# Row halves in MLA, four quarters in RWKV-7, DA's rotation by exchanged loads, moved squares and fills in a two-layer mixer kernel

## Chip, cores and metric

One core of one Trainium2 chip. The metric is the time of one execution of the whole program in device microseconds, the median of several runs. TensorE (PE) multiplies matrices, VectorE (DVE), ScalarE (ACT) and GpSimd (POOL) work element by element, and SyncE (SP) issues DMAs. Each engine works through its own instructions in order; semaphores order the engines among each other.

## What is computed

Two layers over x of 512 tokens by 2048, all in float32. Cut from the reference:

```python
for l in range(DEPTH):                      # 2
    h = rms_norm(x, norm_g[l])
    p = h @ w_in[l]                         # 2048 columns of z, and four groups of heads
    z, p_rw, p_ml, p_mla, p_da = _split(p, IN_WIDTHS)
    y = concat(beta0 * rwkv7(p_rw), beta1 * mlstm(p_ml), beta2 * mla(p_mla), beta3 * diff_attn(p_da))
    x = x + (y * silu(z)) @ w_out[l]
# mla: q, k = [128 columns, 64 rotary columns]; softmax(q k^T, causal) v
# diff_attn: q, k = 2 maps of 64 columns per head, the first 16 columns of each rotated:
def apply_rope(x, cos, sin):
    x1, x2 = x[..., :half], x[..., half:]
    return jnp.concatenate([x1 * c - x2 * s, x2 * c + x1 * s], axis=-1)
# rwkv7, per step: S = S w + (S kk)(kk a) + v k;  y = S r   (done in chunks of 64 tokens)
```

## The kernel before

**The large products.** `x @ w_in` (256 steps a layer: 16 groups of 512 columns by 16 slices of k) and `y @ w_out` (64 steps, in column blocks of 512) are three products each of a high and a low part in fp32r: high by high, low by high, high by low. SP loads a step's weights (`raw`, L711), POOL makes the high part (`w_hi`, L728; in the first groups and the last steps of a layer ACT does, L1228, `high_part`) and the low part (`w_lo`, L738). A step's four tiles (m = 0 to 3) are three matmuls of 128x512 each, into the four banks of `ps_proj` (L769 for `w_in`, L784 for `w_out`).

**The fills.** The four mixers (MLA `la`, RWKV-7 `rw`, mLSTM `ml`, differential attention `da`, in this order, in each layer) run beside the large products. Wherever PE would wait in a mixer, `fill(name, h)` puts in so many tiles of the large products; the table `FILL` gives the counts, `planned()` deals the tiles out in order, so that a tile more here is one less elsewhere. ACT and DVE run the same plan: where a tile is the last of its group, ACT copies the bank out (L1218 `evacuate`, store L1221), and where it is the last of a column block of `w_out`, DVE adds it to x (L1644 `add_tile`). The first tile of the next group or column block waits for that copy or addition. The first three quarters of k of `w_out` run inside the DA stage, in four column blocks of 12 steps.

**Places that the change touches.**
- Start of layer 0 (L835, L1276 to L1335, L1667 to L1698): x arrives in four loads (L693), ACT squares each tile of 128 tokens in two halves (L1276), DVE and ACT make the roots, PE spreads them (L839), DVE scales the turned x, ACT and DVE split it, and the first product of `w_in` (L769) can start. The first `high_part` comes after the first `h_hi`.
- MLA, per head (L904 to L925): scores are, for each of four tiles i of 128 queries, a product over 128 rows (L919), one over the 64 rotary rows (L920, rows `own` = the half of the head) and a mask product in bf16 (L921). All have 128(i+1) columns but the mask (128).
- RWKV-7, for each pair of heads (hp = 0 to 3) (L945 to L1102): the factors (DVE) are turned (L956 to L958), copied out by ACT (L1455 to L1457), v is turned (L963), gram products (L974), the first [gk v] products (L992, two quarters of the array), five levels of an inverse (L1010 to L1031), the last of which is L1038 to L1040, then [a, state term] (L1047, `ps[q, h]`, again on the two quarters q to q), copied by ACT for both heads (L1483), then 96 small matmuls of the chunks' insides (L1057 to L1074, 192 records) and the states, one chunk after another (L1084, fill `rw_state` between).
- DA, per head (L1153 to L1189): sums of squares (L1160, L1162), a product of q and of k with the rotation matrix (L1164, L1165), DVE's multiplication by sine and cosine (L1965 to L1970), scores in two halves (L1176), ACT's exponentials (L1591), DVE's sums (L1982, L1983), then turned (L880).

An f32 matmul stands in the trace as two records.

Of the kernel before, what the change touches and what calls it, by code (L numbers as in the profile page):

```python
# [86 lines left out]
def tiles_of(g):  # L87
# [9 lines left out]
    begin=4, la_first=36, la_sums=18, la_v=4, la_heads=(7, 7, 7, 7), la_qk=(15, 11, 12, 11),  # L97
    la_probs=(13, 13, 13, 13), la_turned=(3, 3, 3, 3), la_gate=(4, 4, 4, 4),
    rw_first=8, rw_lora=(10, 10, 10, 9), rw_factors=(31, 31, 31, 33), rw_turned=(4, 4, 4, 4), rw_v=(2, 2, 2, 2),
    rw_gram=(4, 4, 4, 4), rw_x=(2, 2, 2, 2), rw_level=(1, 1, 1, 1), rw_step=(1, 1, 1, 1), rw_levels=(1, 1, 1, 1),  # L100
    rw_pu=(1, 1, 1, 1), rw_local=(5, 5, 5, 5), rw_state=(1, 1, 1, 1), rw_state_last=(1, 1, 1, 1),
    rw_carried=(2, 2, 2, 2), rw_mean=(3, 3, 3, 3), rw_gate=(13, 14, 13, 12),
    ml_first=25, ml_qk=(15, 10, 10, 10), ml_s=(8, 7, 7, 6), ml_h=(14, 13, 12, 11), ml_gate=(12, 12, 12, 12),
    da_first=21, da_sums=(14, 10, 10, 10), da_scores=(6, 6, 6, 6), da_half=(12, 17, 18, 15), da_turned=(3, 3, 3, 3),
# [4 lines left out]
for _name, _n in (("rw_mu", 13), ("rw_w0", 4), ("rw_a0", 4), ("rw_v0", 4), ("rw_k_k", 4), ("rw_k_a", 4),  # L109
                  ("rw_r_k", 4), ("rw_ln_w", 4), ("rw_ln_b", 4), ("ml_conv_w", 32), ("ml_conv_b", 8),  # L110
                  ("ml_norm_g", 4), ("mla_q_norm_g", 3), ("mla_kv_norm_g", 2), ("mla_q_g", 2),
                  ("mla_k_g", 2), ("da_q_g", 1), ("da_k_g", 1), ("da_sub_g", 1), ("norm_g", 16),
# [8 lines left out]
for _name, _n in (("ident", P), ("ones", P), ("bones", P), ("eps", 2),  # L121
# [3 lines left out]
                  ("rot_da", P), ("cos_da", T), ("sin_da", T),  # L125
# [6 lines left out]
LA_CONST = (CONST["rot_mla"][0], CONST["rot_da"][0])  # L132
DA_CONST = (CONST["rot_da"][0], CONST["causal"][0])
ML_CONST = (CONST["causal"][0], N_CONST)


def constants():
# [43 lines left out]
    put("rot_da", rotation(P, 8, 64))  # L181
    cs, sn = tables(16)
    cd, sd = np.ones((P, T), np.float32), np.zeros((P, T), np.float32)
    for b in (0, 64):
        cd[b:b + 16], sd[b:b + 16] = np.concatenate([cs, cs]), np.concatenate([sn, sn])
# [15 lines left out]
def parameters(given):  # L201
# [8 lines left out]
    for layer in range(DEPTH):  # L210
# [10 lines left out]
        for name in ("da_q_g", "da_k_g"):  # L221
            for half in range(2):
                put(name, layer, given[name][layer:layer + 1], 64 * half)
        for at, name in ((0, "ml_i_b"), (32, "ml_f_b")):
            put("gate_bias", layer, given[name][layer:layer + 1], at)
# [6 lines left out]
def planned():  # L232
# [27 lines left out]
    for h in range(4):  # L260
# [8 lines left out]
        for name in ("rw_levels", "rw_pu", "rw_local"):  # L269
            place(name, h)  # L270
# [47 lines left out]
def build(nc, a, out):  # L318

    with ExitStack() as ctx:  # L320
# [141 lines left out]
        la_mx, la_sum = rg(NT), rg(NT)  # L462
        rot_mla = const("rot_mla", la_const, LA_CONST[0])
# [5 lines left out]
        rot_da = const("rot_da", da_const, DA_CONST[0])  # L469
# [9 lines left out]
        da_qk = carve(da_p_at, 2, T)  # L479
        da_a = rg(NT, T)  # L480
# [166 lines left out]
        s_da_rotated = sem("da_rotated")  # L647
# [29 lines left out]
        for layer in range(DEPTH + 1):  # L677
# [9 lines left out]
            with nc.Block() as block:  # L687
# [54 lines left out]
                def _(pe):  # L742
# [88 lines left out]
                    for k in range(4):  # L831
                        for i in range(NT):
                            if not tail and k == 0:
                                pe.wait_ge(s_x_loaded[i], 16)
# [1192 lines left out]
```

## Time and profile before

| | |
|---|---|
| median of 3 runs | 2431.85 us (2427.43 to 2432.5) |
| the profiled execution's own time | 2427.41 us |
| its span, first to last instruction | 2425.6 us |
| PE busy | 2351.5 us (97%) |
| POOL busy | 1732.2 us (71%) |
| DVE busy | 1158.1 us (48%) |
| ACT busy | 634.4 us (26%) |
| mean granted TensorE clock | 0.993 |
| DMA, mean over the span | 117 GB/s |

The page gives for each engine the time in which it had an instruction in flight. Matmuls are pipelined, so the time that one takes is read from start to start.

### The profile page before, as it was taken

The numbers are of one execution on the slowest core, as the hardware profiler recorded it, in microseconds if no ns is written. First come the engines' busy times: TensorE is split into PE (matmuls) and PEld (weight loads), VectorE is DVE, ScalarE is ACT, GpSimd is POOL, SyncE is SP. The second block draws the span as 40 slices with busy tenths as digits, with TensorE's granted clock in tenths as the row PEclk, the third lists the DMA queues.
The fourth block names the chain that finished last, engine by engine and source line by source line (L and its number), as shares of the span: only waits on it lengthen the run. The fifth ranks groups of instructions, "written<-read, shape, count | busy, mean of one in ns | idle before, by whom it ended". The sixth has DMA issues, their size and how long they took to land. (4 is left out here: it accounts for less than half of the span.)

```text
span 2425.6 us, 38853 instructions
## 1 busy us (share of the span) xinstructions
PE 2351.5 (97%) x16320; PEld 1770.0 (73%) x16320; DVE 1158.1 (48%) x1505; ACT 634.4 (26%) x1124; POOL 1732.2 (71%) x1228
## 2 busy tenths in 40 slices
PE   7999999999999999999999999999999999999999
PEld 5767677777777677777777677777777777777777
DVE  5123345557463675454250232466475547745442
ACT  4222222121221222333241223222122212324321
POOL 3676688668587778777637666877596787888774
PEclk9999999999999999999999999999999999999999
DMA  4623243233233435632445232533232243474223
GB/s 153 189 78 100 79 152 117 75 89 104 81 105 119 127 111 192 218 86 68 140 110 166 79 109 88 157 97 97 67 113 84 84 142 112 133 252 140 79 73 123
DMA packets 163568, 284.18 MB, mean 117 GB/s; under 512 B 28408, under 2 KB 35960, under 8 KB 161856
## 3 DMA queue, kind: packets, MB, share of 16 engines
q1 hardware_dynamic: 108352, 180.93, 26.6%
q10 hardware_dynamic: 55040, 100.77, 12.1%
q8 instruction: 128, 2.10, 0.4%
q14 instruction: 48, 0.39, 0.0%
HBM read 229.97 MB, written 51.64 MB: 116 GB/s over the span
## 5 line engine op out<-in xcount | busy, mean ns | idle before, releaser
L728 POOL TENSOR_SCALAR w_hi<-raw 128x512 fp32r<-128x512 f32 x552 | 903.7, 1637 | 490.8 <-PE ps_proj L769 404.7
L738 POOL TENSOR_TENSOR w_lo<-raw,w_hi 128x512 fp32r<-128x512 f32 (+1 forms) x640 | 832.8, 1302 | 155.0 <-ACT w_hi L1228 99.5
L769 PE MATMUL ps_proj<-h_hi,w_hi 128*128 128x512 f32 (+1 forms) x1760 | 734.8, 418 | 8.0 <-ACT stage L1218 5.0
L769 PE MATMUL ps_proj<-h_lo,w_hi 128*128 128x512 f32 (+1 forms) x1760 | 690.0, 392 | 0.0
L769 PE MATMUL ps_proj<-h_hi,w_lo 128*128 128x512 f32 x1728 | 676.9, 392 | 0.0
L769 PEld LDWEIGHTS ps_proj<-h_hi,w_hi 128*128 128x128 f32 (+1 forms) x1760 | 330.3, 188 | 112.4 <-issue 26.3
L769 PEld LDWEIGHTS ps_proj<-h_lo,w_hi 128*128 128x128 f32 (+1 forms) x1760 | 330.2, 188 | 74.1
L769 PEld LDWEIGHTS ps_proj<-h_hi,w_lo 128*128 128x128 f32 x1728 | 326.3, 189 | 68.7 <-issue 11.1
L784 PE MATMUL ps_proj<-w_hi,h_hi 128*128 128x512 f32 x448 | 184.6, 412 | 9.6 <-DVE arena L1644 9.2
L784 PE MATMUL ps_proj<-w_hi,h_lo 128*128 128x512 f32 x448 | 176.3, 393 | 0.0
L784 PE MATMUL ps_proj<-w_lo,h_hi 128*128 128x512 f32 x448 | 175.8, 392 | 0.0
L784 PEld LDWEIGHTS ps_proj<-w_hi,h_hi 128*128 128x128 f32 x448 | 85.0, 190 | 31.5 <-issue 14.1
L1218 ACT ACTIVATE stage<-ps_proj 128x512 f32<-128x512 f32 (+1 forms) x118 | 70.5, 597 | 136.2 <-PE ps_proj L769 113.8
L769 PE MATMUL ps_proj<-w_hi,h_hi 128*128 128x512 f32 x256 | 104.9, 410 | 0.0
L769 PE MATMUL ps_proj<-w_lo,h_hi 128*128 128x512 f32 x256 | 99.8, 390 | 0.0
L769 PE MATMUL ps_proj<-w_hi,h_lo 128*128 128x512 f32 x256 | 99.8, 390 | 0.0
L784 PEld LDWEIGHTS ps_proj<-w_lo,h_hi 128*128 128x128 f32 x448 | 85.0, 190 | 19.7 <-issue 3.4
L784 PEld LDWEIGHTS ps_proj<-w_hi,h_lo 128*128 128x128 f32 x448 | 84.8, 189 | 18.3
L1717 DVE TENSOR_REDUCE arena<-ps 128x1 f32<-128x128 f32 (+3 forms) x96 | 47.1, 490 | 85.6 <-PE ps L921 60.6
L1228 ACT ACTIVATE w_hi<-raw 128x512 fp32r<-128x512 f32 (+1 forms) x88 | 48.7, 561 | 148.1 <-PE ps_proj L769 75.5
L1263 ACT ACTIVATE arena<-ps 128x512 f32<-128x512 f32 x24 | 14.4, 598 | 242.7 <-PE ps L1102 129.0
L1591 ACT ACTIVATE arena<-ps,arena 128x128 f32<-128x128 f32 (+3 forms) x64 | 38.7, 615 | 129.5 <-DVE arena L1718 129.5
(347 smaller groups left out, 3160.0 us busy)
## 6 DMA issues: line engine op xcount, KB each, us to landing
raw<-in_w_in_dram SPq DMA_DIRECT2D x480, 256.0 KB, 2.7
raw<-in_w_out_dram SPq DMA_DIRECT2D x128, 256.0 KB, 3.0
projected<-stage ACTq DMA_DIRECT2D x116, 256.0 KB, 2.8
arena<-projected ACTq DMA_DIRECT2D x90, 256.0 KB, 3.1
out_dram<-arena ACTq DMA_DIRECT2D x7, 1024.0 KB, 4.8
gated_hi<-arena ACTq DMA_DIRECT2D x24, 256.0 KB, 2.7
gated_lo<-arena ACTq DMA_DIRECT2D x24, 256.0 KB, 3.2
h_hi<-gated_hi SPq DMA_DIRECT2D x8, 768.0 KB, 12.9
```

Of the source, the lines that this page charges most:

```text
L728: nc.gpsimd.tensor_scalar(hi, src, 1.0, None, ALU.mult).then_inc(s_hi_split, 1)
L738: nc.gpsimd.tensor_tensor(lo, src, hi.bitcast(F32), ALU.subtract).then_inc(s_raw_split, 1)
L769: last = mm(ps_proj[rows, m, :], lhsT, rhs, start=(k == 0 and j == 0), stop=(k == KT - 1 and j == len(products) - 1))
L784: last = mm(bank[:, i, :], lhsT, rhs, start=(first and j == 0), stop=(last_k and j == 2))
L1218: nc.scalar.activation(stage[0:rows, m, :], ps_proj[0:rows, m, :], ACT.Copy).then_inc(s_proj_copied, 1)
L1228: nc.scalar.activation(w_hi[:, at_all % N_SPLIT, 0:width], raw[:, at_all % N_RAW, 0:width], ACT.Copy).then_inc(s_hi_by_act, 1)
L1263: link(nc.scalar.activation(dst, src, ACT.Ln, scale=1.0 / n, bias=eps))
L1591: nc.scalar.activation(da_p[:, b, 0:(i + 1) * P], ps[:, b, 0:(i + 1) * P], ACT.Exp, scale=da_rq[:, 4 * half + b:4 * half + b + 1], bias=da ...
L1717: link(v.tensor_reduce(mx[:, b:b + 1], ps[:, b, 0:(i + 1) * P], AX, MAX))
```

## The change

1. MLA: the rotary products of a head's four query tiles come in one block behind the four main products, two of them on the head's own half of the rows and two on the other half, for which DVE copies the rotated q across (`la_qs`), and `la_kp` is made on all rows. The four mask products come last.
2. RWKV-7: [a, state term] and the first [gk v] run on all four quarters of the array, for which the second head's turned factors are copied with their halves exchanged (three ACT copies for one); the last level loses its product with the identity; [a, state term] of the two heads is copied by ACT and DVE, one each; a fill stands between the two halves of the chunks' insides (`rw_outer`).
3. DA: no product with the rotation matrix. ACT loads the exchanged rows with four small DMAs per head (`load_da_swapped`), for the next head ahead of the exponentials of the second half; DVE multiplies them by a signed sine and an exchanged gain.
4. Start of layer 0: x is turned tile by tile; the first tile's squares come before the wait for the constants, the first `high_part` before the copies of the mean.
5. ACT's tanh of the RWKV-7 lora comes ahead of the fill `to_k`; PE turns v after the first of ACT's copies; `FILL` has other counts.

```diff
-    la_qk=(15, 11, 12, 11), rw_factors=(31, 31, 31, 33), rw_turned=(4, 4, 4, 4), rw_pu=(1, 1, 1, 1), rw_local=(5, 5, 5, 5), rw_state_last=(1, 1, 1, 1)
+    la_qk=(17, 11, 13, 11), rw_factors=(31, 33, 33, 33), rw_turned=(3, 3, 3, 3), rw_pu=(2, 2, 2, 2), rw_local=(4, 4, 4, 4), rw_outer=(1, 1, 1, 1), rw_state_last=(0, 0, 0, 0)
-    ml_qk=(15, 10, 10, 10), ml_h=(14, 13, 12, 11), ml_gate=(12, 12, 12, 12), da_half=(12, 17, 18, 15)
+    ml_qk=(19, 10, 10, 10), ml_h=(14, 14, 13, 11), ml_gate=(7, 12, 12, 12), da_half=(12, 17, 15, 16)
...
                             mm(ps[:, i, ks], la_q[:, qs], la_k[:, ks], start=True, stop=False)
-                            mm(ps[:, i, ks], la_qp[own, qs], la_kp[own, ks], start=False, stop=False)
+                        for i, rows, q_pe in ((0, own, la_qp), (1, other, la_qs), (3, own, la_qp), (2, other, la_qs)):
+                            qs, ks = slice(i * P, (i + 1) * P), slice(0, (i + 1) * P)
+                            mm(ps[:, i, ks], q_pe[rows, qs], la_kp[rows, ks], start=False, stop=False)
+                        for i in range(NT):
+                            qs = slice(i * P, (i + 1) * P)
                             mm(ps[:, i, qs], mask_ident, neg, start=False, stop=True).then_inc(s_scores_mm, 1)
...
+                            for lower, upper in ((slice(0, 64), slice(64, P)), (slice(64, P), slice(0, 64))):
+                                link(v.tensor_copy(la_qs[lower, :], la_qp[upper, :]))
...
-                        pe.wait_ge(s_rw_turned_copied, 3 * hp + 3)
+                        pe.wait_ge(s_rw_turned_copied, 3 * hp + 1)
...
+                            for q, o in swapped:
+                                mm(ps[q, 2, own], rw_gk[q, i, 0:64], rw_vT[q, i, 0:64], start=True, stop=True)
+                                mm(ps[o, 3, 256 + i * 64:256 + (i + 1) * 64], rw_gk[q, 4 + i, 0:64], rw_vT[q, i, 64:P],
+                                   start=True, stop=True)
...
-                                mm(ps[o, 3, own], ident[q, q], rw_xt[q, 4 + i, :], start=True, stop=False)
-                                last = mm(ps[o, 3, own], rw_y[q, 4 + i, :], rw_xt[q, 4 + i, :], start=False, stop=True)
+                                last = mm(ps[q, 3, own], rw_y[q, 4 + i, :], rw_xt[q, 4 + i, :], start=True, stop=True)
...
+                            for q, o in swapped:
+                                mm(ps[q, 0, i * P:(i + 1) * P], rw_xt[q, i, :], rw_abv[q, i, 0, :], start=True, stop=True)
+                                last = mm(ps[o, 1, i * P:(i + 1) * P], rw_xt[q, 4 + i, :], rw_abv[q, i, 1, :],
+                                          start=True, stop=True)
...
-                        mm(ps[:, 2, :], rot_da, da_g[:, 0, :], start=True, stop=True)
-                        mm(ps[:, 3, :], rot_da, da_g[:, 1, :], start=True, stop=True).then_inc(s_da_rotated, 1)
...
+                    if not tail:
+                        act.wait_ge(s_x_loaded[0], 16)
+                        for half in range(2):
+                            square_x(0, half, D // 2)
...
+                    if not tail:
+                        high_part(base)
                     for n, tiles in enumerate(ROWS_OF_MEAN):
                         copy_mean(n, tiles)
...
+                    act.wait_ge(s_rw_shifted, 1)
+                    nc.scalar.activation(rw_lora[0:32, 1:T + 1], rw_lora[0:32, 1:T + 1], ACT.Tanh).then_inc(s_rw_lora_tanh, 1)
                     fill("to_k")
...
+                        link(nc.scalar.activation(rw_abv[:, :, 0, 0:64], turned_ar[:, :, 0, :], ACT.Copy))
+                        link(nc.scalar.activation(rw_abv[0:64, :, 1, 0:64], turned_ar[64:P, :, 1, :], ACT.Copy))
+                        nc.scalar.activation(rw_abv[64:P, :, 1, 0:64], turned_ar[0:64, :, 1, :], ACT.Copy).then_inc(s_rw_turned_copied, 1)
...
+                    def load_da_swapped(h):
+                        for b in (0, 64):
+                            for to, of in ((b, b + 8), (b + 8, b)):
+                                act.dma_start(da_sw[to:to + 8], p_dram[4 * G_DAQ + h:4 * G_DAK + h + 1:4, of:of + 8].rearrange("s p t -> p s t")
+                                              ).then_inc(s_da_swapped, 16)
...
                             act.wait_ge(s_da_row_max, 2 * h + half + 1)
+                            if half and h < HEADS - 1:
+                                load_da_swapped(h + 1)
...
                     for h in range(HEADS):
-                        link(v.tensor_tensor(da_qk, ps[:, 2:4, :], wide_sin, MUL))
+                        dve.wait_ge(s_da_swapped, 64 * (h + 1))
+                        link(v.scalar_tensor_tensor(out=da_qk[:, 0, :], in0=da_sw[:, 0, :], scalar=col("da_q_g_swapped"), in1=sin_da, op0=MUL, op1=MUL))
+                        link(v.scalar_tensor_tensor(out=da_qk[:, 1, :], in0=da_sw[:, 1, :], scalar=col("da_k_g_swapped"), in1=sin_da, op0=MUL, op1=MUL))
```

With the new counts, the third and fourth column block of `w_out` begin with the fill `da_turned` of heads 2 and 3, as the first two do. Before, they began inside `da_half`: behind tile 15 of 18 of head 2 and 13 of 15 of head 3. The last tiles of the group `z` of mLSTM's gates lie in `ml_h` of head 0; before, the fourth lay in `ml_gate`.

## Rows read from the trace of the kernel before

**Rows 1.** The page: busy time, share of the span and instructions of each engine.
```profile
PE 2351.5 (97%) x16320; PEld 1770.0 (73%) x16320; DVE 1158.1 (48%) x1505; ACT 634.4 (26%) x1124; POOL 1732.2 (71%) x1228
```
**Rows 2.** PE's waits: waiter and releaser, us in total, times, longest.
```profile
PE ps_proj L784 <- DVE arena L1644: 9.2, 4, 2.6
PE ps L1127 <- DVE arena L1923: 6.4, 4, 2.8
PE ps_proj L769 <- ACT stage L1218: 5.0, 2, 2.5
PE ps L956 <- DVE arena L1820: 4.4, 5, 1.7
PE ps L1074 <- issue: 3.4, 3, 1.2
PE ps L945 <- ACT arena L1432: 3.2, 1, 3.2
```
**Rows 3.** Windows: stretch, us, busy us of each engine (instructions), PEclk, DMA, GB/s.
```profile
2334.90:2341.70 6.80, 6.15 (x20) 5.20 (x21) 2.30 (x4) 1.08 (x3) 1.52 (x2) 0.50 0.25 70
2001.30:2004.70 3.40, 3.40 (x14) 2.38 (x15) 0.94 (x2) 1.59 (x5) 0.97 (x1) 1.00 0.52 170
```
**Rows 4.** Timeline of PE, mLSTM head 0: start us, us, instruction, shape, count.
```profile
808.46 2.32 PE L1135 MATMUL ps<-arena 128*128 128x512 f32 x8
810.61 2.32 PE L1138 MATMUL ps<-arena,always 128*128 128x512 f32 x8
```
**Rows 5.** Timeline of PE, MLA head 0, scores: first product, last two.
```profile
182.89 0.41 PE L919 MATMUL ps<-arena 128*128 128x128 f32 x2
...
187.69 1.12 PE L920 MATMUL ps<-arena 64*128 64x512 f32 x2
188.75 0.23 PE L921 MATMUL ps<-neg,mask_ident 128*128 128x128 bf16 x1
```
**Rows 6.** Timeline, DA head 0, 256-column scores on two row halves, then masks.
```profile
975.79 0.70 PE L1176 MATMUL ps<-arena 64*128 64x256 f32 x4
976.43 0.28 PE L1178 MATMUL ps<-neg,mask_ident 128*128 128x128 bf16 x2
```
**Rows 7.** Timeline of PE, RWKV-7 pair 1: gram products (four quarters), [a, state term] (two).
```profile
508.88 1.98 PE L974 MATMUL ps<-arena 64*64 64x128 f32 x64
...
535.96 1.97 PE L1047 MATMUL ps<-arena 64*64 64x128 f32 x32
```
**Rows 8.** Timeline of PE, RWKV-7 pair 1: states with one tile of fill between.
```profile
546.88 0.33 PE L1084 MATMUL ps<-arena 64*64 64x64 f32 x4
...
548.04 0.33 PE L1084 MATMUL ps<-arena 64*64 64x64 f32 x4
```
**Rows 9.** Timeline of DVE, RWKV-7 pair 1: what the first state product waits for.
```profile
546.50 0.11 DVE L1864 MEMSET arena<- 128x64 f32 x1
```
**Rows 10.** One line's instructions: ns from first to last of the issue on ACT's queue.
```profile
L1556 ACTq DMA_DIRECT2D arena<-projected x8: 450/474/723, 953.6 to 2245.7; - x8
```
**Rows 11.** Timeline of DVE, DA heads 1 and 2: the last sum before the turn.
```profile
1039.35 0.98 DVE L1983 SCALAR_TENSOR_TENSOR arena<-arena 128x512 f32<-128x512 f32 x1
...
1085.06 1.64 DVE L1983 SCALAR_TENSOR_TENSOR arena<-arena 128x512 f32<-128x512 f32 x1
```
**Rows 12.** Timeline of PE, DA heads 1 and 2: the turn; first tile of column block 2.
```profile
1040.98 1.25 PE L880 MATMUL ps<-always,arena 128*128 128x128 f32 x10
...
1087.44 0.46 PE L784 MATMUL ps_proj<-w_hi,h_hi 128*128 128x512 f32 x1 [1.97 <-DVE arena L1644]
```
**Rows 13.** One line's DMAs (x, L693): time from issue to landing.
```profile
DMA to landing us min/median/max: 5.4/8.9/12.1
```
**Rows 14.** Timeline, start of layer 0: ACT's first square, its first high part, PE's first large product.
```profile
9.27 1.06 ACT L1276 ACTIVATE arena<-arena 128x1024 f32<-128x1024 f32 x1
...
22.32 0.62 ACT L1228 ACTIVATE w_hi<-raw 128x512 fp32r<-128x512 f32 x1
...
24.42 0.80 PE L769 MATMUL ps_proj<-h_hi,w_hi 128*128 128x512 f32 x1 [1.44 <-POOL w_lo L738]
```

More of the change, by code:

```diff
@@ L223, in parameters @@
                 put(name, layer, given[name][layer:layer + 1], 64 * half)
+                put(name + "_swapped", layer, given[name][layer:layer + 1, SWAPPED], 64 * half)
         for at, name in ((0, "ml_i_b"), (32, "ml_f_b")):
@@ L268, in planned @@
                 place("rw_step", h, j)
-        for name in ("rw_levels", "rw_pu", "rw_local"):
+        for name in ("rw_levels", "rw_pu", "rw_outer", "rw_local"):
             place(name, h)
@@ L462, in build @@
         la_mx, la_sum = rg(NT), rg(NT)
+        la_qs = rg(T)
         rot_mla = const("rot_mla", la_const, LA_CONST[0])
@@ L830, in _ @@
                         pe.wait_ge(s_setup, 32)
[L831 to L834, printed above, removed]
+                    for i in range(NT):
+                        if not tail:
+                            pe.wait_ge(s_x_loaded[i], 16)
+                        for k in range(4):
                             last = turn(ps[:, k, i * P:(i + 1) * P], x_tok[:, i, k * P:(k + 1) * P], ident)
-                        last.then_inc(s_x_turned, 1)
+                            if i == NT - 1:
+                                last.then_inc(s_x_turned, 1)
                     for n, tiles in enumerate(ROWS_OF_MEAN):
@@ L1064, in _ @@
                                    start=False, stop=True)
+                        fill("rw_outer", hp)
                         for i in range(NT):
@@ L1480, in _ @@
                         fill("rw_levels", hp)
-                        for h in range(2):
-                            act.wait_ge(s_rw_pu_mm, 2 * hp + h + 1)
-                            nc.scalar.activation(rw_pu[:, 4 * h:4 * h + 4, :], ps[:, h, :].rearrange("p (i c) -> p i c", i=NT), ACT.Copy).then_inc(s_rw_pu_ready, 1)
+                        act.wait_ge(s_rw_pu_mm, hp + 1)
+                        nc.scalar.activation(rw_pu[:, 0:4, :], ps[:, 0, :].rearrange("p (i c) -> p i c", i=NT), ACT.Copy).then_inc(s_rw_pu_ready, 1)
                         fill("rw_pu", hp)
+                        fill("rw_outer", hp)
                         act.wait_ge(s_rw_local, hp + 1)
```

87 lines of the change are left out of this document (41 added, 46 removed).

## The prediction

> **What bounds the kernel now.** I began with the page's busy line: PE has an instruction in flight for 97% of the span, the next engine, POOL, for 71% [rows 1]. So the first question to each edit is what it takes from PE's own stream, and only then what it does to waits. The second view is the list of PE's waits: six entries, 31.6 us together [rows 2], most of them where a bank of the large products must be copied out or added before the next tile. The third is the table of windows with the granted clock: behind one wait PE ran 6.8 us at 0.50, that is at 1.2 GHz, twice 3.4 us, and did half the work in it, while the stretch behind the wait at 2001 us shows 1.00, 2.4 GHz [rows 3]. The last is the timeline of PE around each place. A large product moved by `FILL` costs PE the same wherever it stands, so the counts matter by the waits they cover alone. The reader should keep apart in the sum: work that disappears (firm) and waits that move (soft).
>
> **1. DA's rotations go.** A product of 128 rows has 512 columns here and mLSTM's block of four such products, 1280 columns, took 810.61 − 808.46 = 2.15 us [rows 4], 1.68 ns a column. Two of 512 columns are 1.72 us, and there are 8 heads in the two layers: −13.7 (−13.5 to −14).
>
> **2. MLA.** A head's scores ran from 182.89 to 188.75 plus a mask, some 5.9 us, with a row-half product of 512 columns at 1.06 us, as long as a whole one [rows 5]. New: four 128-row products, 2.15 as in [rows 4]; then rotary products in pairs. DA's two row halves of 256 columns went together, 0.64 us for the four records [rows 6], against 2 × 0.43 in turn at 1.68 ns. Each half carries 128 + 512 and 256 + 384 columns in all, 640 per half: 1.1 us at that rate, 1.3 with 0.2 for the unequal pairs and the switch; masks 0.3. Sum 3.8, so −2.1 a head, −16.8. If the halves don't overlap it is about −1.05 a head. Range −8.4 to −17.5. DVE's two copies for `la_qs` are 64x512 each, taken at 1.1 to 1.6 us like DVE's 512-column operations [rows 11]; `la_qk` has two tiles more for head 0 and one more for head 2 to cover them; uncovered they cost up to 1 us a head, in the range of part 5.
>
> **3. RWKV-7.** [a, state term] took 1.97 us for 32 records on two quarters; the gram products had 64 records in 1.98 on four [rows 7]. On four quarters the 32 take about 1.05 with switching: −0.9 + 0.05, −0.85 × 8 pairs = −6.8. The first [gk v] has a third of that: −0.3 × 8 = −2.4. The last level without its identity product loses a third of its records but stays on two quarters: −0.1 × 8 = −0.8. Sum −10.0 (−0.8 to −12).
>
> **4. Start of layer 0.** A load of x lands at the earliest 5.4 us after issue [rows 13], but the first square started at 9.27 and the first large product at 24.42, with its low part, which needs the high part at 22.32, landing last [rows 14]. Squares of tile 0 ahead of the constants' wait and the high part ahead of the mean's copies bring the chain 2 to 4 us forward; part of PE's work there runs at 1.2 GHz anyway. I take −3.5 (−1.5 to −4.5).
>
> **5. Waits that the counts cover.** In [rows 2]: L784 on DVE's addition, 9.2 in four waits: with the column block changed inside `da_turned` the turn (1.25 us busy [rows 12]) stands between, all −9.2. L1127, 6.4: `ml_qk` 15 to 19 in head 0 is four tiles of 0.69 us, 2.75 a layer against waits of at most 2.8: −5.5. L769 on ACT's evacuation, 5.0: the fourth z tile goes ahead of ACT's root: −5.0. L956, 4.4: two tiles more for pairs 1 and 2: −3.0. L945, 3.2: tanh now ahead of `to_k`, but DVE's chain is next late: −1.9. Sum −24.6 (−18 to −26).
>
> **6. The clock.** The low stretches that follow such waits cost 1.7 us for each 3.4 us [rows 3]. I found some ten in the trace, six behind waits that go in part 5: −10.2; but waits of the same size elsewhere, 2001 us among them [rows 3], were followed by none, and new waits (8) may bring some, +1.9. I take −8.3 (0 to −12).
>
> **7. Issue.** PE waited 3.4 us for nothing but its own sequencer at L1074 [rows 2], within the 192 records of the chunks' insides; counted from start to start, five of eight such blocks took about 4.4 instead of 3.0 us. `rw_outer` splits them with a tile of fill, in which the sequencer can run ahead: −5.5 (−9 to +1, as the split may shift the stall only). The split itself switches the array's shape twice: the states with a tile between them come every 1.16 us, for 0.69 of tile and 0.11 of states [rows 8], so 0.36 is the switch: +0.36 × 8 = +2.9 (+2 to +3.5).
>
> **8. The added issues on ACT.** DA's next-head loads are four DMA issues on ACT, which stand in its queue ahead of the exponentials of the second half; behind those wait DVE's sums and PE's turn. One issue on that queue took 0.45 to 0.72 us [rows 10]; 0.33 for the first and three of 0.46, 1.75 in all, is my value; the exchanged rows are small descriptors, so up to 2.9 by the longest. Head 0: covered by an evacuation that PE awaits anyway. Head 1: DVE's last sum ended 1040.33, PE's turn began 1040.98 [rows 11, 12]; 0.65 of slack less some 0.05 of semaphore, so 1.75 − 0.6 = +1.15. Head 2: ended 1086.70; PE would have been there at 1087.44 − its wait of 1.97 = 1085.47 with 18 tiles [rows 12]. That wait goes (part 5), but PE now arrives with 15 tiles, three of them moved behind the turn, so the turn itself waits for 1086.70 + 1.75 = 1088.45, near 3.0. Head 3: no loads. Sum 4.2 × 2 layers = +8.5 (+3 to +18; the low end if DVE's chain, which loses its sums of the rotated products, is that much sooner).
>
> **9. Other small new waits.** `rw_local` 5 to 4: PE comes 0.69 sooner than 546.88 [rows 8], at 546.19, and DVE's clear ends at 546.61 [rows 9]: +0.5 × 8 = +3.9. `rw_turned` 4 to 3 with three of ACT's copies before the last turned factors: +1.9. `ml_gate` 12 to 7 in head 0: +2.0. Sum +7.8 (+3 to +11).
>
> At nothing: DVE's two products for the rotation replace one over both banks, and DVE is at 48% [rows 1]; a tile more or less elsewhere; POOL, which at 71% [rows 1] is not late for PE but in the start.
>
> **Rules weighed.** Before the change [a, state term] wrote both row halves into one bank `ps[q, h]` and ran at half the rate of the gram products [rows 7]. The Trainium skill ("TensorEngine Tiling (Array Packing)", Gotcha 1: PSUM Pressure) says that different row tiles cannot use one PSUM bank at the same time. The new code puts the halves of a pair in different banks in RWKV-7, and in MLA i = 0 and 1, 3 and 2 go to four banks, so by this rule all overlap. Its other side is a rival below. A second rule speaks against MLA's order. There the pairs are unequal (128 beside 256 columns, 512 beside 384). The Trainium skill ("TensorE: Matmul & The Clock Gate", on packing) has matmuls start strictly in order; by it the shorter of a pair leaves its half idle, some 0.3 us a head, +2.6 in all, and the sum would be 2.6 above mine. I keep 0.2 a head for it.
>
> **The sum.** −13.7 − 16.8 − 10.0 − 3.5 − 24.6 − 8.3 − 5.5 + 2.9 + 8.5 + 7.8 = −63.2, say −64 with the small wait at mLSTM's next heads that `ml_gate` frees. The profiled execution's own time is 2427.4, so 2363; the runs' median stands 4.4 above it, so **2367** as a median of runs.
>
> **Rivals.**
> - *The cover is lost* (0.20): work goes, but the waits are re-made elsewhere. Then part 6 gives 0 (+8.3), part 5 its low end (+6.6), part 8 the longest issue of [rows 10] in heads 1 and 2 (+1.15 × 4 = +4.6), part 7 half (+2.8): +22, 2389. For it: equal waits with and without a slow stretch [rows 3]; six fills shrink. Against: the firm parts stay.
> - *The halves don't overlap* (0.10): if banks or read ports of the row halves serialise, MLA gives −8.4 instead of −16.8, and RWKV-7 −0.8 instead of −10.0: +17.6, 2385. For it: [rows 7], two quarters at half rate. Against: [rows 6], whose row halves go at once.
> - *Fewer new waits* (0.07): parts 8 and 9 at their low ends, −10, and issue at −9: 2353.
> - *No difference* (0.03): what goes is off the path. Against: PE at 97% [rows 1].
> - *Slower* (0.02): the exchanged loads. They are the only long step added in a chain ahead of PE, ACT's queue in DA. The gain of 64 is used up if each of the six batches holds the turn 10.7 us longer than in part 8, that is from 12.5 us a batch or 3.1 an issue on, against at most 0.72 in [rows 10]; or if landing is late: the loads have a head's time, 46 us from turn to turn [rows 12], against 12.1 at most for x [rows 13].
> - The forecast has 0.58.
>
> Range: 2352 (fewer new waits) to 2391 (lost cover, with a little more), leaving out no difference, slower and the tails. A measurement of this kernel tells about 0.2% from no change: faster 0.95, within 0.2% 0.03, slower 0.02.
>
> **What would show it.** MLA's block near 3.8 us and [a, state term] near 1.05 in PE's timeline (parts 2, 3); no L1164 and L1165; PE's busy time down by some 45; the waits of [rows 2] on L1644, L1218 and L1432 gone or small; L1127 short; PE's wait for `issue` gone; new waits at the turn of DA's heads 1 and 2 of 1.1 and 3.0, and of 0.5 at L1084; first L769 about 20.5 instead of 24.42; fewer windows at 0.50. I am wrong if the row halves show records in turn, if low stretches are as many as before, or if the turn waits for ACT longer than 3 us.

## The result, and the profile after

The changed kernel takes 2415.1 us in the median (2414.1 to 2418.2), the kernel before beside it 2432.2 (2427.4 to 2434.5): ratio 0.9938, 95% interval 0.9924 to 0.9952. That is faster, by 15 us going by the ratio, but I had forecast 2367 with a range of 2352 to 2391: the direction held, the size did not. 49 us of the gain are missing, and the question of this document is where they went. Its profiled execution took 2416.05 us, with a span of 2414.3, so 11.3 us less than the span before.

The page's busy line of the changed kernel, which answers to [rows 1]:

```profile
PE 2324.0 (96%) x16160; PEld 1751.9 (73%) x16160; DVE 1192.2 (49%) x1515; ACT 634.9 (26%) x1133; POOL 1737.8 (72%) x1228
```

PE is busy 27.5 us less, while the span is only 11.3 shorter: the other 16 us are new idle time of PE. The list of PE's waits of the changed kernel, to be laid beside [rows 2] (waiter and releaser, us in total, times, longest):

```profile
PE ps L1185 <- DVE arena L1999: 22.9, 4, 11.5
PE ps L886 <- DVE arena L2012: 11.4, 8, 1.5
...
PE ps L1131 <- DVE arena L1659: 5.9, 2, 2.9
PE ps L963 <- DVE arena L1817: 5.0, 3, 2.1
...
PE ps L1095 <- DVE arena L1889: 3.2, 8, 0.4
...
PE ps L1138 <- DVE arena L1948: 1.1, 2, 0.6
...
PE ps L967 <- DVE arena L1850: 0.9, 3, 0.3
```

All waits of [rows 2] are gone or short, as forecast (L1138 is the old L1127, L967 the old L956). Four others stand at the head. L886 is the turn in DA, L1131 the first product of an mLSTM head, L963 the product for RWKV-7's kk, L1095 the state. The first line is the largest by far and stands in no step of the forecast: the first scores of DA's head 0, twice some ten us. What the engines did there (timelines of ACT, of DVE and of PE; start us, us; ACTq is ACT's issue):

```profile
939.51 0.46 ACTq L1595 DMA_DIRECT2D arena<-in_x_dram  x1
...
945.83 2.21 ACTq L1579 DMA_DIRECT2D stage<-projected  x4
```
```profile
965.29 0.96 DVE L1992 SCALAR_TENSOR_TENSOR arena<-stage,par,arena 128x512 f32<-128x512 f32 x1 [29.04 <-DMA stage<-projected]
966.29 0.75 DVE L1993 SCALAR_TENSOR_TENSOR arena<-stage,par,arena 128x512 f32<-128x512 f32 x1
967.08 2.17 DVE L1995 TENSOR_TENSOR arena<-arena 128x1024 f32<-128x1024 f32 x1
```
```profile
971.49 0.80 PE L1185 MATMUL ps<-arena 64*128 64x128 f32 x4 [11.47 <-DVE arena L1999]
```

The four exchanged loads of 32 KB, issued from 945.8 us on, were there only at 965.2, 19 us later, and PE stood from 960.0 on. Six us ahead of them in the same queue is the load of x for the later additions, 4 MB. The same stretch in the view of DMAs (939 to 966 us; KB each, median us from issue to landing):

```profile
arena<-in_x_dram ACTq DMA_DIRECT2D x1, 4096.0 KB, 19.1
h_hi<-gated_hi SPq DMA_DIRECT2D x3, 768.0 KB, 16.1
...
arena<-projected ACTq DMA_DIRECT2D x3, 256.0 KB, 17.3
raw<-in_w_out_dram SPq DMA_DIRECT2D x3, 256.0 KB, 13.8
```

What is issued in this stretch lands 13.8 to 19.1 us after its issue, on ACT's queue and on SP's, but for one load of constants just ahead of x (6.6). In the kernel before, x (19.4) and the loads behind it (15.1 on ACT's queue, 16.6 and 21.3 for h on SP's) were about as late, but nothing on PE's way depended on them.

The granted clock (windows as in [rows 3]): the idle stretches of the changed kernel are followed, or accompanied, by 1.2 GHz.

```profile
962.16:975.81 13.65, 4.32 (x17) 2.87 (x18) 7.51 (x11) 0.00 (x0) 2.98 (x2) 0.50 0.94 342
818.80:825.63 6.83, 6.83 (x17) 4.30 (x14) 5.78 (x9) 2.66 (x4) 2.28 (x2) 0.50 0.75 244
2163.65:2173.89 10.24, 5.67 (x20) 3.93 (x21) 5.97 (x10) 1.26 (x5) 2.42 (x2) 0.50 0.94 346
```

The firm parts came as forecast. MLA's scores in head 0 of the changed kernel, beside [rows 5]:

```profile
183.56 2.42 PE L926 MATMUL ps<-arena 128*128 128x128 f32 x8 [0.70 <-DVE arena L1764]
185.91 1.35 PE L929 MATMUL ps<-arena 64*128 64x128 f32 x8
187.19 0.40 PE L932 MATMUL ps<-neg,mask_ident 128*128 128x128 bf16 x4
...
187.40 0.47 PE L774 MATMUL ps_proj<-h_hi,w_hi 128*128 128x512 f32 x1
```

183.56 to 187.40 is 3.84 us, forecast 3.8; the eight rotary records, two halves of the rows at once, take 1.28 (forecast 1.3). And [a, state term], beside [rows 7]:

```profile
428.17 0.32 PE L1057 MATMUL ps<-arena 64*64 64x128 f32 x1
...
429.01 0.27 PE L1058 MATMUL ps<-arena 64*64 64x128 f32 x1
429.20 0.50 PE L774 MATMUL ps_proj<-h_hi,w_hi 128*128 128x512 f32 x1
```

32 records in 1.03 us, forecast 1.05.

### The profile page after: what moved, and what is told of

It reads as the page before. It is cut to its first block and busy times, and to the rows that moved or that the text cites. A ratio compares the mean times of both kernels' runs of the same rounds, so it can differ in the third digit from the quotient of the medians.

```text
span 2414.3 us, 38594 instructions
## 1 busy us (share of the span) xinstructions
PE 2324.0 (96%) x16160; PEld 1751.9 (73%) x16160; DVE 1192.2 (49%) x1515; ACT 634.9 (26%) x1133; POOL 1737.8 (72%) x1228
## 5 line engine op out<-in xcount | busy, mean ns | idle before, releaser
L774 PE MATMUL ps_proj<-h_hi,w_hi 128*128 128x512 f32 (+1 forms) x1760 | 740.1, 421 | 2.0 <-POOL w_lo L743 0.9
L774 PE MATMUL ps_proj<-h_lo,w_hi 128*128 128x512 f32 (+1 forms) x1760 | 691.8, 393 | 0.0
L774 PE MATMUL ps_proj<-h_hi,w_lo 128*128 128x512 f32 x1728 | 678.5, 393 | 0.0
L774 PEld LDWEIGHTS ps_proj<-h_hi,w_hi 128*128 128x128 f32 (+1 forms) x1760 | 331.3, 188 | 113.1 <-issue 29.7
L774 PEld LDWEIGHTS ps_proj<-h_lo,w_hi 128*128 128x128 f32 (+1 forms) x1760 | 331.3, 188 | 75.0
L774 PEld LDWEIGHTS ps_proj<-h_hi,w_lo 128*128 128x128 f32 x1728 | 327.8, 190 | 68.6 <-issue 11.4
L789 PE MATMUL ps_proj<-w_hi,h_hi 128*128 128x512 f32 x448 | 181.1, 404 | 0.4 <-POOL w_lo L743 0.4
L789 PE MATMUL ps_proj<-w_hi,h_lo 128*128 128x512 f32 x448 | 174.9, 390 | 0.0
L789 PE MATMUL ps_proj<-w_lo,h_hi 128*128 128x512 f32 x448 | 174.5, 390 | 0.0
L774 PE MATMUL ps_proj<-w_hi,h_hi 128*128 128x512 f32 x256 | 105.6, 412 | 0.2
L774 PE MATMUL ps_proj<-w_lo,h_hi 128*128 128x512 f32 x256 | 100.7, 394 | 0.0
L774 PE MATMUL ps_proj<-w_hi,h_lo 128*128 128x512 f32 x256 | 100.5, 393 | 0.0
L789 PEld LDWEIGHTS ps_proj<-w_hi,h_hi 128*128 128x128 f32 x448 | 84.2, 188 | 19.1 <-issue 1.9
L789 PEld LDWEIGHTS ps_proj<-w_lo,h_hi 128*128 128x128 f32 x448 | 84.3, 188 | 18.3 <-issue 1.9
L789 PEld LDWEIGHTS ps_proj<-w_hi,h_lo 128*128 128x128 f32 x448 | 84.1, 188 | 18.1
## 6 DMA issues: line engine op xcount, KB each, us to landing
h_hi<-gated_hi SPq DMA_DIRECT2D x8, 768.0 KB, 13.7
```

What stands on the lines that cost most here:

```text
L774: last = mm(ps_proj[rows, m, :], lhsT, rhs, start=(k == 0 and j == 0), stop=(k == KT - 1 and j == len(products) - 1))
L789: last = mm(bank[:, i, :], lhsT, rhs, start=(first and j == 0), stop=(last_k and j == 2))
```

## The experiments

Ratios are to the kernel before, with the 95% interval; 0.001 is 2.4 us. "From start to start" means PE's records in the trace, each up to the start of the next, with idle time taken out. The theory I began with: the head-0 loads behind x's 4 MB cost the most; the small waits of L886 and L1131 are the rest. The rival: row loads are slow wherever they stand, or the parts of the change themselves do not reach the end.

**xlast: the load of x behind the exchanged loads.**

```diff
-                    act.dma_start(x_tok, x_dram ...)
                     fill("to_z_da")
                     square_qk(0)
...
                     load_da_swapped(0)
+                    act.dma_start(x_tok, x_dram ...)
```

> The changed kernel with one thing moved: ACT issues the load of x (4 MB, for the later additions) behind the exchanged loads of DA's head 0 instead of ahead of them. In the changed kernel PE waits 11.5 and 9.8 us for DVE at the first scores of DA's head 0, since the exchanged rows, issued at 946 us, are there only at 965. Theory (they stand behind the 4 MB in the DMA queues): rows there before 957, that wait under 1 us in both layers, the slow-clock stretches around it gone (some 5 us), the time some 27 us below the changed kernel, about 2388, ratio to before 0.982. Rival (loads of single rows take 15 us and more wherever they stand): the wait stays above 8 us, ratio 0.993.

Measured: 2397.9 us, 0.9875 (0.986 to 0.989), 15 us below the changed kernel. DVE's timeline in xlast:

```profile
951.55 0.75 DVE L1992 SCALAR_TENSOR_TENSOR arena<-stage,par,arena 128x512 f32<-128x512 f32 x1 [18.67 <-DMA stage<-projected]
952.33 1.85 DVE L1993 SCALAR_TENSOR_TENSOR arena<-stage,par,arena 128x512 f32<-128x512 f32 x1
954.22 1.52 DVE L1995 TENSOR_TENSOR arena<-arena 128x1024 f32<-128x1024 f32 x1
955.77 2.22 DVE L1996 TENSOR_TENSOR arena<-arena 128x1024 f32<-128x1024 f32 x1
```

The rows are there at 951.5, 9 us after their issue at 942.6 instead of 19. So the cause is that they were issued behind x's 4 MB, and the rival (single rows are slow wherever they stand) falls. Whether it is the place in ACT's queue or the load on the DMA engines in that stretch (loads on SP's queue were about as late), no run separates. But the wait did not fall under 1 us: 2.6 and 2.9 us stay, since DVE's six operations behind the landing take 7.6 us (951.55 to 959.2; 6.1 in the changed kernel), which I had not counted. So 15 us instead of the 27 expected.

**lateswap: xlast, and the next head's exchanged loads behind the exponentials.**

```diff
                             act.wait_ge(s_da_row_max, 2 * h + half + 1)
-                            if half and h < HEADS - 1:
-                                load_da_swapped(h + 1)
...
                         tanh_z(12 + h, da_z, da_e)
+                        if h < HEADS - 1:
+                            load_da_swapped(h + 1)
```

> xlast, and the exchanged loads for the next head are issued behind the second half's exponentials and z's tanh instead of ahead of the exponentials. Theory (the four issues, 1.34 us, delay exponentials, DVE's sums and PE's turn): PE's wait at the turn, 1.5, 1.5 and 1.4 us in heads 0 to 2, falls to 0.8, 0.1 and 0.1, head 3 (no loads) stays at 1.3; 6 us below xlast, ratio about 0.9795. Rival (the turn waits because three tiles went from in front of it and DVE's operations are longer): waits stay above 1 us, time as xlast.

Measured: 2395.2 us, 0.9861 (0.9846 to 0.9876); the intervals of the two overlap, so by time alone some 3 us are only likely. PE's waits show it plainly: head 0 from 1.49 to 0.78 (now for ACT's copy-out, as before the change), head 1 from 1.50 to nothing; head 2 from 1.40 to 1.28 and head 3 from 1.27 to 1.28. The expectation held for heads 0 and 1 and failed for head 2. ACT's timeline of head 1 in the changed kernel shows the cost of the issues:

```profile
1030.62 1.35 ACTq L1579 DMA_DIRECT2D stage<-projected  x4
1032.01 0.67 ACT L1619 ACTIVATE arena<-ps,arena 128x384 f32<-128x384 f32 x1 [7.69 <-issue]
```

Four issues, 1.35 us (forecast 1.75), and the exponentials begin 1.39 us later. In heads 2 and 3 the wait is the same with and without issues: it comes of PE's early arrival. In head 2 three tiles stand behind the turn instead of in front of it, and in both heads the wait for DVE's addition that held PE up ahead of the turn is gone (dahalf below brings both back, and these waits go).

**norot: the rotation by products again, all else as changed.**

```diff
+                        mm(ps[:, 2, :], rot_da, da_g[:, 0, :], start=True, stop=True)
+                        mm(ps[:, 3, :], rot_da, da_g[:, 1, :], start=True, stop=True).then_inc(s_da_rotated, 1)
                         fill("da_sums", h)
...
-                    load_da_swapped(0)
...
-                                load_da_swapped(h + 1)
```

> The changed kernel with DA's rotation undone: products with the rotation matrix as before, no exchanged loads; all other parts and the counts as changed. Theory (the exchanged loads lost more than the products cost): 11.2 us of products come back, the waits of 22.9 us at head 0, 5 us of slow clock and some 7 us at the turn go: 24 us below the changed kernel, ratio about 0.983. Rival (the exchanged loads are a gain and the lost time is elsewhere): above the changed kernel by 5 us or more, ratio 0.996.

Measured: 2394.5 us, 0.9861 (0.9844 to 0.9877), 19 us below the changed kernel; expected 24. The products return 11.2 us from start to start (7.5 and 3.7 for the two lines; 13.7 with what they add to the tile behind them, see step 1 below), PE's idle time falls by 27.8. So within this change the exchanged loads are a loss of 19 us, and even in lateswap's order they only draw level. Only in best1's order (below) are they a gain: best1 differs from norot in nothing but the rotation's way and the place of two loads beside it, and it is 14 us faster (0.9804 against 0.9861, intervals apart), as much as the products cost.

**mlfill: mLSTM's head 0 with the counts of before, but for one tile** (`ml_gate` 11 instead of 12).

```diff
-    ml_qk=(19, 10, 10, 10), ml_gate=(7, 12, 12, 12)
+    ml_qk=(15, 10, 10, 10), ml_gate=(11, 12, 12, 12)
```

> The changed kernel with mLSTM's head 0 counts as before but for one tile: ml_qk 15 instead of 19, ml_gate 11 instead of 7 (the sum is kept, so all later tiles stand where they stood). Theory (a tile covers one wait or the other, not both): the wait of 2.9 us at the next head's first product goes in both layers (-5.9) with the two slow-clock stretches of 6.8 us there (-6.8), and the scores' wait (+5.3), the wait for the copy-out of z's banks (+5.0) and one or two slow stretches (+1.7 to +3.4) come back: within 4 us of the changed kernel, ratio 0.992 to 0.996. Rival (the moved counts are a gain of 10 us as forecast): ratio 0.998.

Measured: 2419.0 us, 0.9959 (0.9945 to 0.9973), as expected, if near its upper end. Two lines of its waits:

```profile
PE ps L1138 <- DVE arena L1948: 6.1, 4, 2.7
PE ps_proj L774 <- ACT stage L1227: 5.3, 2, 2.8
```

The wait at L1131 of 5.9 is gone, and 5.0 at L1138 and 5.3 at the copy-out have come back. By the ratios the four moved tiles are worth some 5 us, of the 10 that I had counted; the two intervals touch (up to 0.9952, from 0.9945), so the sign is likely and the size loose.

**best1: lateswap, the cosine ahead of the wait, the exchanged loads ahead of z's.**

```diff
                     for h in range(HEADS):
+                        dve.wait_ge(s_da_squared, h + 1)
+                        link(v.tensor_tensor(da_g, da_g, cos_da[:, None, :].to_broadcast([P, 2, T]), MUL))
                         dve.wait_ge(s_da_swapped, 64 * (h + 1))
...
-                    load_z(12, da_z)
                     act.wait_ge(s_da_cleared, 1)
                     load_da_swapped(0)
+                    load_z(12, da_z)
```

> lateswap, with two more moves for DA's head 0: DVE multiplies by the cosine before it waits for the exchanged rows, and these are issued ahead of the load of z as well. In xlast the rows were there at 951.5 and DVE's chain behind them took 7.6 us, of which 1.5 to 2.2 are the cosine. Theory (the chain from the rows' landing still ends last): the wait of 2.6 and 2.9 us goes to 0 to 1 in both layers and the slow stretches behind it go: 4 to 7 us below lateswap, ratio 0.9835. Rival (the chain from the sums and ACT's roots ends last by then): the wait stays above 2 us, ratio 0.986.

Measured: 2383.7 us, 0.9804 (0.9788 to 0.982): 11 to 14 us below lateswap, more than expected. In its timelines the cosine is done before, and PE doesn't wait:

```profile
943.83 1.45 DVE L1992 TENSOR_TENSOR arena<-arena 128x1024 f32<-128x1024 f32 x1 [8.77 <-DMA arena<-in_const_dram]
953.52 0.75 DVE L1994 SCALAR_TENSOR_TENSOR arena<-stage,par,arena 128x512 f32<-128x512 f32 x1 [8.24 <-DMA stage<-projected]
954.31 0.98 DVE L1995 SCALAR_TENSOR_TENSOR arena<-stage,par,arena 128x512 f32<-128x512 f32 x1
```
```profile
958.88 0.49 PE L1185 MATMUL ps<-arena 64*128 64x128 f32 x4
```

Putting the loads ahead of z's brought nothing by itself (landing at 953.5); the work taken out of the chain did. Of the 11.8 us between the two profiled spans, 6.2 are idle time, 5.6 of it at L1185; and 4.6 are slow clock (27 us at 1.2 GHz in lateswap, 17 in best1, of which PE loses half of what it works in them: 13.1 and 8.5).

**noouter and best2: no tile between the halves of the chunks' insides**, on the changed kernel and on best1.

```diff
-    rw_local=(4, 4, 4, 4), rw_outer=(1, 1, 1, 1)
+    rw_local=(5, 5, 5, 5), rw_outer=(0, 0, 0, 0)
```

> The changed kernel with rw_outer 0 and rw_local 5 instead of 1 and 4: the tile that splits the chunks' insides stands behind them again. Theory of the forecast (the split lets PE's sequencer run ahead): idle time put down to issue in these 192 records comes back, some 7 us in all, the 0.36 us of switching per pair goes (-2.9), PE's wait at the states (3.2) goes: about 1 us above the changed kernel, ratio 0.994. Rival (the idle time went for another cause): none comes back, 6 us below the changed kernel, ratio 0.9915.

> best1 with rw_outer 0 and rw_local 5: no tile between the halves of the chunks' insides. Against the changed kernel the same edit gave 7 us with a wide interval. Theory (the split costs eight times a switch of the array's shape, 0.26 us by the traces, and a wait of 0.4 us at the states, 5.3 in all, and saves 3.6 of issue): 1 to 4 us below best1, ratio 0.979 to 0.980. Rival (all 7 us are the split's): ratio 0.9775.

Measured: noouter 2407.9 us, 0.9909 (0.9887 to 0.9931), 7 us below the changed kernel with wide intervals; best2 2381.9, 0.9795 (0.978 to 0.981), against best1's 0.9804: no difference that the intervals tell. Some issue idle does come back in noouter:

```profile
PE ps_proj L774 <- issue: 1.6, 2, 1.0
PE ps L1079 <- issue: 1.4, 1, 1.4
PE ps L1082 <- issue: 1.3, 1, 1.3
PE ps L1085 <- issue: 1.0, 1, 1.0
```

5.3 us, against 3.2 of the wait at L1095 that goes and the array's switching. The split is worth nothing, and probably costs a little. Of the 8.0 us between the profiled spans of noouter and the changed kernel, 6.2 are slow clock (10.5 us lost to it instead of 16.7), which need not be the split's doing. Of the 5.5 that I had booked for it, what it adds elsewhere takes all.

**nomla: MLA's scores as before.**

```diff
                             mm(ps[:, i, ks], la_q[:, qs], la_k[:, ks], start=True, stop=False)
+                            mm(ps[:, i, ks], la_qp[own, qs], la_kp[own, ks], start=False, stop=False)
-                        for i, rows, q_pe in ((0, own, la_qp), (1, other, la_qs), (3, own, la_qp), (2, other, la_qs)):
-                            mm(ps[:, i, ks], q_pe[rows, qs], la_kp[rows, ks], start=False, stop=False)
```

> The changed kernel with MLA's scores as before: each tile's rotary product on the head's own rows behind its main product, no la_qs, la_kp on the own rows. In the traces the block is 5.9 us before and 3.9 after. Theory (all of that reaches the end): 17 us above the changed kernel, ratio 1.001. Rival (a shorter block only lets PE arrive sooner at waits in MLA): at most 8 us above, ratio 0.997 or less.

Measured: 2428.5 us, 0.9995 (0.9985 to 1.0004): 14 us above the changed kernel; 17 were forecast, and 17.1 are there from start to start. The profiled spans are 13.1 apart: in nomla 3.3 us less are lost to slow clock, and PE is idle 0.9 less.

**norw: RWKV-7's products as before.**

```diff
-                                mm(ps[q, 0, i * P:(i + 1) * P], rw_xt[q, i, :], rw_abv[q, i, 0, :], start=True, stop=True)
-                                last = mm(ps[o, 1, i * P:(i + 1) * P], rw_xt[q, 4 + i, :], rw_abv[q, i, 1, :], ...)
+                                    last = mm(ps[q, h, i * P:(i + 1) * P], rw_xt[q, 4 * h + i, :], rw_abv[q, i, h, :], ...)
```

> The changed kernel with RWKV-7's products as before: [gk v] and [a, state term] on two quarters, last level with the identity product, one ACT copy of the turned factors, one engine copying [a, state term]; counts and rw_outer as changed. By PE's start-to-start times these parts take 9.5 us less after. Theory (they reach the end): 9 to 10 us above the changed kernel, ratio 0.9977. Rival (the three ACT copies and the changed order make new waits, which take it back): within 4 us of the changed kernel, ratio 0.9955 or less.

Measured: 2428.8 us, 0.9994 (0.9984 to 1.0003), 14 us above the changed kernel, where 9 to 10 were expected. The theory holds, the rival falls: this part reaches the end in full. The profiled spans are 11.3 apart, 9.6 of it PE's own products, 2.0 a longer wait of PE for ACT before v is turned.

**dahalf and nostart: two small parts undone on best1.**

```diff
-    da_half=(12, 17, 15, 16)
+    da_half=(12, 17, 18, 15)
```

> best1 with da_half (12, 17, 18, 15) as before the change: the third and fourth column blocks of w_out begin inside da_half again. Theory (the moved block starts are a gain, less what the turn now waits): four waits for DVE's addition of 2.0 to 2.6 us come back (+9), the waits of 1.3 us at the turn of heads 2 and 3 go (-5), up to three slow-clock stretches come back (+5): 4 to 9 us above best1, ratio 0.982 to 0.984. Rival (the wait only changes its place, with nothing gained): as best1, 0.9804.

Measured: 2393.7 us, 0.9846 (0.9831 to 0.9861), 10 us above best1. All four waits for DVE's addition came back, 9.2 us in all as in [rows 2], those at the turn of 5.1 went, and three slow stretches stand right behind the 2.0- to 2.6-us waits. This part is a gain of 10 us. In the profiled executions (dahalf's was 4 us above its median) idle time is 4.7 us of the difference and slow clock 12.0 (20.5 us lost instead of 8.5), so the larger half of it is the clock, not the waits themselves.

nostart (the four edits of the start taken back):

```diff
-                    if not tail:
-                        act.wait_ge(s_x_loaded[0], 16)
-                        for half in range(2):
-                            square_x(0, half, D // 2)
...
-                    if not tail:
-                        high_part(base)
```

> best1 with the start of layer 0 as before: x turned k by k, first squares behind the wait for the constants, first high part behind the copies of the mean. In the traces the first large product started at 24.4 us before and at 22.1 after. Theory: 2.3 us and the slow-clock stretch at 20 us (2.1) come back, 4 us above best1, ratio 0.982. Rival (POOL's low parts set the pace of the first tiles, so the earlier first product is lost again within layer 0's first group): within 1.5 us of best1, ratio 0.9804 to 0.981.

Measured: 2387.4 us, 0.9818 (0.9805 to 0.9831) against best1's 0.9804: 3.4 us by the ratios, the intervals overlap. Its size fits, its sign is likely and not shown.

**best3: best2 with counts moved from long slack to short.**

```diff
-    la_qk=(17, 11, 13, 11), ml_qk=(19, 10, 10, 10), ml_h=(14, 14, 13, 11), ml_gate=(7, 12, 12, 12)
+    la_qk=(18, 11, 13, 10), ml_qk=(17, 10, 10, 10), ml_h=(14, 13, 13, 11), ml_gate=(10, 12, 12, 12)
```

> best2 with tiles taken from where PE comes long after its signal and given to where it waits: la_qk (18, 11, 13, 10), ml_qk head 0 17 instead of 19, ml_h head 1 13 instead of 14, ml_gate head 0 10 instead of 7. Theory: the wait at mLSTM's second head, 2.95 us, falls to 0.9 in both layers (-4.1), the slow stretches behind it go (-3.4 to -5), MLA's wait of 0.7 goes (-1.4), the scores of head 0 wait 0.8 (+1.6): 7 to 9 us below best2. Rival (waits of under 1 us bring slow stretches as well, or the copy-out of z comes late): within 3 us of best2.

Measured: 2381.0 us, 0.9796 (0.9783 to 0.981), as best2: my theory failed. Three tiles (2.1 us) moved in front of L1131 shortened its wait by 0.4 only:

```profile
816.07 0.69 PE L1131 MATMUL ps<-arena 36*128 36x512 f32 x1 [2.54 <-DVE arena L1659]
```

ACT's timelines say why, the changed kernel's first, then best3's:

```profile
809.24 0.60 ACT L1227 ACTIVATE stage<-ps_proj 128x512 f32<-128x512 f32 x1 [0.46 <-ACT stage L1227]
...
810.22 1.28 ACT L1272 ACT_TABLE_LOAD   x1 [0.39 <-ACT stage L1227]
```
```profile
805.66 1.02 PE L1156 MATMUL ps<-arena,always 128*128 128x512 f32 x2
```
```profile
806.59 0.60 ACT L1227 ACTIVATE stage<-ps_proj 128x512 f32<-128x512 f32 x1 [0.46 <-ACT stage L1227]
...
807.58 1.28 ACT L1272 ACT_TABLE_LOAD   x1 [0.39 <-ACT stage L1227]
```

The tiles shifted the end of the group, so four copy-outs, 1.06 us apart, now end behind PE's product (start 805.66), and ACT's root with its table load begins 1.9 us after that start, not 0.5 (809.69 in the changed kernel). What a tile gives in front of the wait it takes from the chain that the wait is for.

## Why the prediction was wrong, step by step

**1, DA's products**: −13.7 forecast, and right. The two lines' own records are 11.2 us from start to start, but the first record of the tile behind them also takes 0.63 us where it takes 0.32 without them. From the start of the sums of squares to the second record of that tile, before and then in the changed kernel:

```profile
962.90 0.95 PE L1162 MATMUL ps<-always,arena 128*128 128x2 f32 x8
...
965.74 0.39 PE L769 MATMUL ps_proj<-w_lo,h_hi 128*128 128x512 f32 x1
```
```profile
949.42 0.95 PE L1173 MATMUL ps<-always,arena 128*128 128x2 f32 x8
...
950.54 0.39 PE L774 MATMUL ps_proj<-w_lo,h_hi 128*128 128x512 f32 x1
```

2.84 us against 1.12: 1.7 a head, and the same in all eight. The sum below goes by lines and so has 11.2 here and the other 2.5 as a gain within the large products.

**2, MLA**: −16.8 forecast, −17.1 in the trace, 14 by nomla. **3, RWKV-7**: −10.0 forecast, −9.5 in the trace, 14 by norw. Both right, but for a small term: the last level without its identity product gives 0.1 in all, not 0.8. MLA's rotary block took 1.28 us where 640 columns at 1.68 ns are 1.08, so the 0.2 a head that was kept for the unequal pairs is what they cost, with no 2.6 us on top. The rival "the halves don't overlap" is refuted for both: 1.28 us and 1.03 us are the times of work at once. On the banks the forecast misread its own code: in RWKV-7 `ps[q, 0]` and `ps[o, 1]` are each written by both halves of the rows, as `ps[q, h]` was before. What changed is the number of quarters, two to four, and the old half rate was that. Both halves write into one bank, on different partitions, all the time, so here the trace does not agree with the full width of the rule in the Trainium skill ("TensorEngine Tiling (Array Packing)", Gotcha 1: PSUM Pressure); whether both may write the same partitions of a bank was not tried.

**4, the start**: −3.5 forecast. The first large product started at 22.09 instead of 24.42; the stretch up to MLA got 1.7 us shorter in all, nostart says 3.4 with overlapping intervals. In its range.

**5, the waits covered**: the waits named went, by 27 us (L789's −9.2, confirmed by dahalf; L774's −5.8, L1138's −5.3, L967's −3.5, L956's −3.2). But two came in their place. L963 waits 5.0: before, PE stood 3.2 us for the tanh up to 371.04; now it passes there at 361 and stands at the next place where DVE's same chain ends,

```profile
371.44 1.04 PE L963 MATMUL ps<-arena,always 128*128 128x512 f32 x1 [2.14 <-DVE arena L1817]
```

I had named this follower but set it at 1.3 for a single place, where it is 2.1; it also appears at pair 3 of both layers with 1.4. And L1131's 5.9 I had at 2.0 in step 9.

**6, the clock**: −8.3 forecast, +1.5 found. Before, 34 us of the span were at 1.2 GHz, after, 48, in which PE worked 30.5 and 33.4 us, at half speed. The stretches that I saw going went, and the new waits (L1131, L963, L1185) brought others: as much low clock as before was one of the forecast's own signs of being wrong. Single executions differ here: L963's wait of 2.1 us was followed by a slow stretch in the changed kernel and by none in best1, and the executions of the kernel before had granted clocks of 0.990 to 0.995, so some us of this term are luck. In best2, with fewer waits of over 2 us, 4.8 us are lost to it, where the kernel before lost 15.2: this term was real, but hung on the others.

**7, issue**: idle for issue fell from 7.2 us to 0.7, as forecast, and the split's own costs took it back (noouter, best2): 3.2 of wait at L1095, and some 2 for the switches and the tile's slower start, where +2.9 was forecast.

**8, the added issues**: +8.5 forecast, +9.8 found at the turn, so the sum was right, but the split by head was not: 1.5, 1.5, 1.4, 1.3 instead of 0, 1.15, 3.0, 0. Head 3's I had called 0: before, a column block began inside its `da_half`, and the wait of 2.6 us for DVE's addition had hidden that PE came early at the turn. When a wait is taken away, what it covered becomes visible.

**The step that failed**: the transfer of head 0's exchanged rows, a wait that the forecast put at nothing. It stands in no part of the sum and only in the rival "Slower". I took the head's 46 us between turns as the time a load has, and compared it with 12.1 us of a load of x at the start [rows 13]. Both hold for heads 1 to 3, where the loads were in time. For head 0 neither does: it has 14 us from issue to PE's arrival (945.8 to 960.0), and stands behind 4 MB in one of the busiest stretches. I had its issue in the "slower" rival, and never looked at what is issued ahead of it. Cost: 24 us of idle time at L1185 and about 5 of slow clock; xlast, lateswap and best1 give back 33 us together, though some of that is head 1's issues.

**9, small new waits**: +7.8 forecast; L1095 3.2 (forecast 3.9, though its own rows give 546.61 − 546.19 = 0.42 a pair, 3.4 in all), the fewer tiles of `rw_turned` +0.8 at L974 (1.9), L1113 +1.1 (not forecast), L1131 +5.9 (2.0).

**What no step had**: the large products' own time rose by 6.7 us from start to start, with the same count, 0.4 of it the clock, and that net of the 2.5 of step 1. In MLA, 2.2 and 2.3 us a layer. A timeline of PE's weight loads in the changed kernel:

```profile
233.16 0.19 PEld L774 LDWEIGHTS ps_proj<-h_hi,w_hi 128*128 128x128 f32 x1 [0.47 <-ACT stage L1227]
...
234.21 0.19 PEld L774 LDWEIGHTS ps_proj<-h_hi,w_hi 128*128 128x128 f32 x1 [0.53 <-ACT stage L1227]
```

A tile takes PE 0.69 us, but where it must wait for ACT's copy-out of its bank, they come every 1.05 us, and this stands in no list of PE's waits, since PE's last matmul is counted as busy almost all the while. Tiles held up inside a group like this cost 4.7 us more than before over the whole span; the rest of the rise stays open. So the forecast's premise, that a large product costs PE the same wherever it stands, does not hold. I moved `la_qk`'s counts at nothing, and they moved these ends of groups to a place with ACT busy. That they are the reason is argued from the place alone: no run takes them back.

Put together from the trace, roughly: −37.8 (products) −1.7 −27 −6.5 is −73; +24.3 (head 0), +9.8 (turn), +5.9, +5.0, +3.2, +1.1, +0.9 (the switch in front of the split's tile), +1.5 (clock), +6.3 (large products) and some 3 of waits under 1 us bring it to −12, against −11.3 measured between the spans. best2 at −50 us shows that forecast's −65 was too high by some 15 even with head 0 mended: by the traces those are mainly L1131, L963 and the copy-outs.

## What to carry to other kernels

When a change adds a load, write down for its first use what is issued ahead of it, on its queue and the others, megabytes included, and how long before the consumer it is issued; an average over later uses says nothing of it. Take each covered wait as the end of a chain and name the next place at which the same chain can end, as the gain is only the difference. And where fills are fixed in number, moving one also moves what the other engines do at the end of its group.

## What the runs showed of the hardware

Four DMAs of 32 KB had landed 19 us after their issue when issued 6 us behind 4 MB on the same queue, and after 9 us ahead of it; on the other queue, loads of 256 and 768 KB issued in the same stretch took 13.8 to 17.2 us. Operations of the same line and shape on DVE took 1.66 and 0.69 us within 3 us of each other (L1781 of the changed kernel, 351.8 and 354.5), so a chain of six can differ by some us from one schedule to another. Products on the two halves of the rows run at once even where they are unequal (MLA: 128 beside 256 and 512 beside 384 columns, 1.28 us for 640 in each half). Two f32 products of 512 columns cost PE 1.71 us although their own records are 1.40 from start to start: the rest shows in the first record of the tile behind them.
